# Sums of squares of three SSD groups formed inside the head loop, and rows of reciprocal roots taken through DRAM

## The reference

```
attn_out = rmsnorm(o.reshape(b, L, 2048), attn_norm_g) * silu(z_attn)      # o: 16 heads x 128
y = (y_f + y_b + d_skip * xs) * silu(z_ssm)                                # SSD, 32 heads x 64
y = rmsnorm(y.reshape(b, L, 4, 512), norm_g.reshape(4, -1))                # a mean of squares per group of 512 columns
mix = concatenate([attn_out, y]) @ w_out
out = x + rmsnorm(mix, post_norm_g)
```

## Time and profile before

| | |
|---|---|
| time, median of 3 executions | 2438.62 us (2438.27 to 2438.85) |
| the profiled execution's own time | 2437.44 us |
| its span, first to last instruction | 2435.6 us |
| granted clock of PE, mean | 0.998 |
| PE busy | 2405.2 us |
| PEld busy | 2284.6 us |
| DVE busy | 1744.1 us |
| ACT busy | 979.5 us |

### The profile page before, as it was taken

How to read it: one execution, slowest core, us unless ns; L and a number is a source line. 1 busy time by engine, 2 the same in 40 slices (tenths; PEclk the granted TensorE clock), 3 DMA queues, 4 the chain that set the end, 5 groups by cost and what they waited for, 6 DMA issues and landing times.

```text
span 2435.6 us, 37103 instructions
## 1 busy us (share of the span) xinstructions
PE 2405.2 (99%) x13708; PEld 2284.6 (94%) x13708; DVE 1744.1 (72%) x2435; ACT 979.5 (40%) x1622; POOL 387.4 (16%) x580
## 2 busy tenths in 40 slices
PE   7999999999999999999999999999999999999998
PEld 6999999999999999999999999999999988888887
DVE  5686766666666655554787888788878768787767
ACT  6323433333333333333445444544454533234332
POOL 0000267666676600000000000000000000000000
PEclk9999999999999999999999999999999999999999
DMA  4235466566556533335464546554654435443544
GB/s 162 78 108 161 132 193 193 185 190 193 185 188 185 179 95 95 99 100 205 145 188 143 180 144 186 171 152 144 193 163 134 143 113 179 156 156 120 170 167 157
DMA packets 316776, 379.43 MB, mean 156 GB/s; under 512 B 20006, under 2 KB 237286, under 8 KB 313751
## 3 DMA queue, kind: packets, MB, share of 16 engines
q1 hardware_dynamic: 265063, 222.06, 29.5%
q10 hardware_dynamic: 33200, 106.02, 13.0%
q0 software_dynamic: 18432, 50.36, 6.4%
HBM read 299.16 MB, written 86.54 MB: 158 GB/s over the span
## 4 chain that ended last, share of the span: by engine, by line
PE 95%; DMA 1%; DVE 1%; ACT 1%; issue 0%; ACTq 0%; SPq 0%; DVEq 0%
PE ps L1029 36%; PE ps L827 21%; PE ps L1182 14%; PE ps L805 8%; PE ps L1102 4%; PE ps L988 2%; PE ps L955 2%; PE ps L922 2%; PE ps L938 1%; PE ps L998 1%; DMA w_raw<-in_w_in 1%; PE ps L760 0%; PE ps L962 0%; PE ps L841 0%; PE ps L929 0%; PE ps L971 0%
## 5 line engine op out<-in xcount | busy, mean ns | idle before, releaser
L1029 PE MATMUL ps<-h_hi,w_hi 128*128 128x384 f32 x960 | 322.2, 336 | 0.0
L1029 PE MATMUL ps<-h_lo,w_hi 128*128 128x384 f32 x960 | 322.0, 335 | 0.0
L1029 PE MATMUL ps<-h_hi,w_lo 128*128 128x384 f32 x960 | 321.7, 335 | 0.0
L2211 DVE TENSOR_TENSOR w_lo<-raw_qk,w_hi 128x512 fp32r<-128x512 f32 x240 | 185.0, 771 | 180.4 <-ACT w_hi L1555 179.3
L827 PE MATMUL ps<-h_hi,w_hi 128*128 128x384 f32 x1056 | 275.1, 341 | 0.0
L1262 ACT ACTIVATE w_hi<-w_raw 128x512 fp32r<-128x512 f32 x176 | 110.0, 628 | 400.7 <-PE ps L827 270.7
L827 PE MATMUL ps<-h_lo,w_hi 128*128 128x384 f32 x1056 | 268.9, 335 | 0.0
L827 PE MATMUL ps<-h_hi,w_lo 128*128 128x384 f32 x1056 | 268.8, 335 | 0.0
L1029 PE MATMUL ps<-t_hi,w_lo 128*128 128x384 f32 x720 | 243.5, 338 | 0.0
L1029 PE MATMUL ps<-t_hi,w_hi 128*128 128x384 f32 x720 | 243.2, 338 | 0.0
L1029 PE MATMUL ps<-t_lo,w_hi 128*128 128x384 f32 x720 | 242.6, 337 | 0.0
(11 more groups left out here) (335 smaller groups left out, 5190.0 us busy)
## 6 DMA issues: line engine op xcount, KB each, us to landing
raw_qk<-in_w_in SPq DMA_DIRECT2D x90, 512.0 KB, 4.3
w_raw<-in_w_in SPq DMA_DIRECT2D x176, 256.0 KB, 3.6
stage<-loc_scr ACTq DMA_DIRECT2D x16, 1536.0 KB, 7.3
stage<-t_scr SPq DMA_DIRECT2D x48, 512.0 KB, 3.6
stage<-in_w_out SPq DMA_DIRECT2D x36, 512.0 KB, 3.5
stage<-zx_scr ACTq DMA_DIRECT2D x46, 384.0 KB, 9.0
stage<-in_w_in SPq DMA_DIRECT2D x30, 512.0 KB, 4.1
u_scr<-stage ACTq DMA_DIRECT2D x32, 384.0 KB, 2.6
```

What stands on the lines that cost most here:

```text
L1029: ins = nc.tensor.matmul(ps[:, bank, 0:HALF_T], w, h(k), start=(start and kk == 0 and q == 0), stop=(last and kk == KC - 1 and q == 2), sk ...
L2211: nc.vector.tensor_tensor(w_lo[:, n_slot(n, pp), :], src, w_hi[:, n_slot(n, pp), :].bitcast(f32), ALU.subtract).then_inc(w_lo_done, 1)
```

## The change

- **Squares in the loop.** For heads 0 to 11 (SSD groups 4, 5, 6), ACT squares y in step 1 of the next head, behind the exponentials of the sample (`square_of_y`): the first head of a group directly into the sum (two instructions), the others into `x_tok` (one instruction). DVE adds the others into the sum in step 2, between `pT_lo` and the decay exponents (`add_square_of_y`, two instructions). Before ACT copies the next x into `x_tok` in step 4 it waits for that addition. The sum lies in the triangles' place of `sq_c` and in `loc_ssum`.
- **Their sums over the partitions.** PE has them in slot 5 of the head behind the group's last (`group_sums`, three times), DVE forms the mean in step 6 (`group_mean`), PE waits for it before the next scores. One square root (ACT) and one reciprocal (DVE) after the last head serve all three.
- **PE's loop.** The iterations before it are 0 to 3, and the body holds four iterations and runs 3 times.
- **Rows.** Each of the four rows is stored to `r_scr` in DRAM (768 numbers from 128 partitions x 6) and loaded to all partitions (`store_root`, `load_root`, both on ACT's queue). `diagonals` and `roots_to_rows` are gone, so is ACT's copy.
- **Squares of group 7** stay where they were, but DVE adds one per unit, units 2 to 5, in place of two in unit 2 and two in unit 3.

```diff
-            def square_first(k):
...
+            def square_of_y(a):
+                if a % 4 == 0:
+                    if a == 0:
+                        for i in range(2):
+                            act.wait_ge(sum_a_out[i], 16 * SUM_TURNS)
+                        act.wait_ge(sum_d_out, 32 * SUM_TURNS)
+                    else:
+                        act.wait_ge(stat_ready, a // 4)
+                    nc.scalar.activation(ysum, y[:, 0:SEQ], ACT.Square)
+                    nc.scalar.activation(ysum_s, y[:, SEQ:T], ACT.Square).then_inc(y_squared, 1)
+                else:
+                    nc.scalar.activation(x_tok, y, ACT.Square).then_inc(y_squared, 1)
...
                 if a is not None and s == 1:
...
+                    if 1 <= a <= 4 * GROUP_STATS:
+                        square_of_y(a - 1)
...
+            def add_square_of_y(a):
+                dve.wait_ge(y_squared, X_DONE + a + 1)
+                did(nc.vector.tensor_tensor(ysum, ysum, x_tok[:, 0:SEQ], ALU.add))
+                nc.vector.tensor_tensor(ysum_s, ysum_s, x_tok[:, SEQ:T], ALU.add).then_inc(ysum_added, 1)
...
+                    if 1 <= a <= 4 * GROUP_STATS and (a - 1) % 4:
+                        add_square_of_y(a - 1)
                     decay_exponents(a)
...
+            def group_sums(g):
+                pe.wait_ge(ysum_added, X_DONE + 3 * g)
+                for t in range(TT):
+                    src = ysum[:, t * P:(t + 1) * P] if t < PCH else ysum_s[:, (t - PCH) * P:(t - PCH + 1) * P]
+                    last = nc.tensor.matmul(ps[:, 4, HALF_T + t:HALF_T + t + 1], src, ones[:, 0:1],
+                                            start=True, stop=True)
+                last.then_inc(stat_ready, 1)
...
-            iteration(1, 1, 0)
-            with pe.Fori(1, HEADS // 2) as g:
-                iteration(2 * g, 0, 2 * g - 1)
-                iteration(2 * g + 1, 1, 2 * g)
+            for i in range(1, 4):
+                iteration(i, i % 2, i - 1)
+            with pe.Fori(1, GROUP_STATS + 1) as g:
+                for q in range(4):
+                    iteration(4 * g + q, q % 2, 4 * g + (q - 1), (q, g))
...
-            def roots_to_rows(n, halves):
...
-            def diagonals(j, n, halves):
...
+            def store_root(j, n, stored):
+                act.wait_ge(r_ready, 1 if j < GROUP_STATS else j - GROUP_STATS + 2)
+                act.dma_start(r_scr[n].rearrange("(t p) -> p t", p=P), r_of(j), allow_slow_non_contiguous=True
+                              ).then_inc(stored, 16)
+            def load_root(n, row, came):
+                act.dma_start(row, r_scr[n:n + 1, :].rearrange("a t -> (a t)").partition_broadcast(P)).then_inc(came, 16)
...
+            store_root(STAT_SECOND, 0, r_stored)
+            store_root(STAT_THIRD, 1, r_stored)
             root(STAT_ATT)
+            store_root(STAT_ATT, 2, r_late_stored)
             w2_split(2)
             w2_split(3)
+            act.wait_ge(r_stored, 32)
+            act.wait_ge(w2_lo_done, 1)
+            load_root(0, r_rows[0], r_row_in)
+            load_root(1, r_rows[1], r_row_in)
+            act.wait_ge(r_late_stored, LATE_STORED + 16)
+            load_root(2, r_att_row, r_late_in)
...
+                    if step == 1 and p == 3 and i >= 2:
+                        add_square(1, 2, i - 2)
-                            if step == 1 and p == 3:
-                                add_square(1, 3, 2, k)
```

More of the change, by code:

```diff
@@ L909, in _, with slot @@
             QK_PASSES = ((q_hi, k_hi), (q_hi, k_lo), (q_lo, k_hi))
-            def slot(s, a, i):
+            def group_sums(g):
[5 more added lines that the diff above has]
+                last.then_inc(stat_ready, 1)
+            def slot(s, a, i, stat=None):
                 if a is not None and s == 0:
+                    if stat is not None and stat[0] == 2:
+                        pe.wait_ge(stat_read, stat[1])
                     pe.wait_ge(tile_out, tile_of(a, K) + 1)
@@ L973, in slot @@
                         last.then_inc(xt_ready, 1)
+                if s == 5 and stat is not None and stat[0] == 1:
+                    pe.wait_ge(xt_out, 2 * a + 2)
+                    group_sums(stat[1])
                 if a is not None and s == 6:
@@ L1108, in sums_of_squares @@
             def sums_of_squares(j):
-                if j == STAT_FIRST:
-                    pe.wait_ge(ssum_ready, 1)
-                elif j == STAT_ATT:
+                if j == STAT_ATT:
                     pe.wait_ge(att_gated, HEADS)
                 else:
[L1114 to L1119, removed]
+                    pe.wait_ge(ssum_ready, 1)
+                    pe.wait_ge(stat_read, STAT_LAST)
                 src = osq_sum if j == STAT_ATT else ssum
-                bank, at = (6, 0) if j == STAT_FIRST else (7, HALF_T)
                 for t in range(TT):
-                    last = nc.tensor.matmul(ps[:, bank, at + t:at + t + 1], src[:, t * P:(t + 1) * P], ones[:, 0:1],
+                    last = nc.tensor.matmul(ps[:, 7, HALF_T + t:HALF_T + t + 1], src[:, t * P:(t + 1) * P], ones[:, 0:1],
                                             start=True, stop=True)
                 last.then_inc(stat_ready, 1)
-            def roots_to_rows(n, halves):
[L1129 to L1132, removed]
             def first_step():
@@ L1688, in _ @@
             w2_split(1)
+            act.wait_ge(stat_read, GROUP_STATS)
+            nc.scalar.activation(r_cur[:, 0:GROUP_STATS, :], r_cur[:, 0:GROUP_STATS, :], ACT.Sqrt).then_inc(r_root, 1)
             store_y(HEADS - 1)
@@ L1693, in root, with squares_of @@
                 nc.scalar.activation(r_of(j), r_of(j), ACT.Sqrt).then_inc(r_root, 1)
-            def diagonals(j, n, halves):
[L1696 to L1707, removed]
+            def store_root(j, n, stored):
[4 more added lines that the diff above has]
+                act.dma_start(row, r_scr[n:n + 1, :].rearrange("a t -> (a t)").partition_broadcast(P)).then_inc(came, 16)
+            def squares_of(n, times):
                 act.wait_ge(u_buf_in[n], X_IN + 16 * times)
+                act.wait_ge(um_done, GRP)
                 for k in range(1, GRP):
-                    act.wait_ge(usq_added, (GRP - 1) * turn + k)
+                    act.wait_ge(usq_added, k)
                     nc.scalar.activation(usq, u_buf[n][:, k * T:(k + 1) * T], ACT.Square).then_inc(usq_done, 1)
@@ L1766, in _ @@
                         a_round(f + 1, h)
+                    if step == 1 and p == 5:
+                        act.wait_ge(r_late_stored, LATE_STORED + 32)
+                        act.wait_ge(um_done, 2 * GRP)
+                        load_root(3, r_rows[2], r_late_in)
                     if step == 1 and p == 3:
-                        squares_of(1, 3, 2)
+                        squares_of(1, 2)
                     for h in range(2, PHASE_B):
@@ L2173, in step @@
                     settle()
+                if s == 6 and a % 4 == 0 and 0 < a <= 4 * GROUP_STATS:
+                    group_mean(a // 4 - 1)
                 if s == 7:
@@ L2501, in _ @@
             mean_and_root(STAT_ATT)
-            for k in range(GRP):
-                add_square(0, 1, 1, k)
             w2_split(2)
@@ L2506, in _ @@
                 first_part(1, t)
-            mean_and_root(STAT_SECOND)
-            for k in range(GRP):
-                add_square(1, 2, 1, k)
             w2_split(3)
@@ L2523, in _ @@
                     for k in range(GRP):
-                        normalise(1, gb, k, row=2)
+                        normalise(1, gb, k, row=1)
                 if t >= 4:
@@ L2556, in _ @@
                             if step == 1 and p == 6:
-                                normalise(1, BLOCK_GROUPS[2][1], k, row=3)
+                                normalise(1, BLOCK_GROUPS[2][1], k, row=2, times=2)
                     if step == 1 and p == 4 and i == 2:
```

127 lines of the change are left out of this document (42 added, 85 removed).

## The result

The changed kernel takes 2449.91 us (median of 6 runs, 2448.84 to 2453.6) against 2438.44 for the kernel before in the same session: a ratio of 1.0054, 95% interval 1.0043 to 1.0064. It is slower by 11.5 us. The forecast was 2441.3, the range 2432 to 2447, with 0.21 on slower.

A forecast was written before the change was run, and what follows sets the result against it. PE, busy 99% of the span, was taken to bound the kernel. Terms of -7.25 (end part), +8.6 (head loop) and +1.3 (branches) gave +2.65 us on 2438.62, so 2441.3 us; range 2432 to 2447.

The forecast's parts named there:

- What PE no longer does: End part: four rows of roots leave PE, 6.35 us less; three sums of squares only move into the head loop, 0 net.
- the stall in the second pair: Second pair at the end: PE's wait for a unit that DVE adds late goes, 0.90 us less.
- The squares and the additions: Head loop: ACT's squares cost PE 5.9 us in 12 heads, DVE's additions 2.7 in nine; 8.6 us more.
- PE's longer loop: Two backward branches of the head loop: PE may fetch the doubled body again; 1.3 us taken between bounds 0 and 4.4.
- The prediction's own sign of being wrong: Head loop: the forecast is wrong if L955 shows no wait, or if either backward branch shows more than 2 us.
- backward branches: Rival, head loop: the body of four does not stay, two branches cost 2.2 us each; 2444.4 us, chance 0.16.
- What is hidden: End part: storing and loading the rows through DRAM costs PE nothing, with about 20 us of room for the first two.
- the rows come late: Rival, end part: storing 768 single numbers takes so long that group 5 is multiplied late; some 2446 us, chance 0.05.

The follow-up runs named there:

- experiment 9: Changed kernel with the edits of experiment 5, experiment 6, experiment 7 and experiment 8 together: 2430.27 us against 2438.03 for the kernel before, ratio 0.997.
- experiment 6: Changed kernel with only DVE's additions of squares moved behind the low part of the sample's probabilities: 2445.86 us against 2438.03 for the kernel before.
- experiment 7: Changed kernel with ACT's squares moved to step 2 and DVE's additions behind the low part of the sample's probabilities: 2439.3 us against 2438.03 before the change.
- experiment 1: Kernel before the change with only PE's loop over heads lengthened to four iterations, three passes: 2444.57 us against 2437.07, ratio 1.0031.
- experiment 2: Kernel before the change with only PE's loop lengthened to three iterations, 1947 PE instructions, four passes: 2449.66 us, ratio 1.0048.
- experiment 8: Changed kernel with the roots of groups 1 and 2 turned on PE and stored as 12 rows of 512 bytes: 2445.26 us against 2437.07 before the change.
- experiment 5: Changed kernel with PE's loop over heads written out in full, no backward branch between heads: 2440.13 us against 2437.07 for the kernel before, ratio 1.0014.

## Why the prediction was wrong

Two steps failed: the branch term was sized too low, and the rows through DRAM were taken as hidden. The method, to read each term from a row, held wherever there was a row of the thing itself. Step by step:

- *What PE no longer does* and *the stall in the second pair*: right. 7.25 us were forecast; experiment 9 has 7.5 for these terms and 7.28 in all. In the changed kernel itself the saving for group 6's row was lost to the wait below.
- *The squares and the additions*: right, 8.11 against 8.6 in sum, and experiments 6 and 7 take them away one by one. Head 0 was a good measure of what lateness costs there.
- *PE's longer loop*: the mechanism was named and the size was wrong. I took 1.3 us for two branches, between bounds of 0 and 4.4; they cost 7.1. Two faults are in that. The upper bound came from the transfer of 80 KB in the earlier trace rows (2.2 us), as if a stop were one such transfer. In experiments 1 and 2 PE stands 2.5 to 3.0 us each time; what that time is made of no run shows. And the value between the bounds leaned on the earlier trace rows, a loop that stays, which says nothing on a loop that doesn't. The lower clock at some of the stops, 1.6 us for a stretch of 3.4 us, I had not thought of at all. The prediction's own sign of being wrong, over 2 us at either branch, came true at both. The rival "backward branches" had the right cause, at 0.16 and with too low a price: with 7.1 in place of 4.4 it gives 2438.6 - 7.25 + 8.6 + 7.1 = 2447.1.
- *What is hidden*: wrong. The stores of 768 single numbers were priced by the row of another transfer. The second took 24.3 us, the load behind it 15.1, together twice the 20 us of room. PE paid 2.5 (the row's 1.29 not saved, 1.24 more) and 0.8 in the first pair, 3.3 in sum. The rival "the rows come late" had 0.05.

The two errors, 5.8 and 3.3 us, make 9.1; between the forecast's +2.65 and the measured +11.4 lie 8.8, as the other terms together came out 0.3 lower.

The Trainium skill (Runtime: NRT & Kernel Launch, Instruction fetch mechanics) says that a taken branch whose target isn't in the current window of two pages forces a fetch of that page before execution goes on. The stops at the branches agree, with 2.4 to 3.8 us each. The window doesn't: by the same section a page is 256 instructions, and the body of 1299 stays. The section's size of 2048 instructions for PE is not the length of a loop that stays either: bodies of 1587, 1779 and 1947 had to be fetched again in every pass. It is not disproved as a size: for 1587 instructions, 6.2 blocks of 256, the queue brings nine packets a pass, so more than the body is fetched. Whether this is why the body's start is no longer there no run shows.

What stays open: why the lower clock follows some stops and not others (1 of 2 in the changed kernel and in experiments 1, 6, 7 and 8, 3 of 3 in experiment 2, 6 of 6 with 1587 instructions, 1 of 6 with 1779); why the stops are 3.4 to 3.8 us with 1587 instructions and 2.4 to 3.0 elsewhere; where between 1299 and 1587 the limit lies; and whether one store of single numbers alone would have come in time.

## What to carry to other kernels

Keep a hardware loop of the bounding engine as short as one that is seen to stay, or write it out in full. Whether it stays is told by the instruction queue in the loop's second pass; if it does not, each backward branch cost a stop of 2.4 to 3.8 us here. Don't price a store of many single numbers by a transfer of another shape: here, beside other such stores and loads of weights, it took 15 to 32 us and held up the loads, and turning two columns to rows first cost PE 0.11 us. Work put on an engine just ahead of a hand-over without room costs most of its length (0.39 to 0.55 us of PE's time for a push of some 0.73 us); the same work behind the hand-over cost nothing.

## What the runs showed of the hardware

- A PE loop of 1299 instructions stays with the engine; of 1587, 1779, 1947 and 2595 (experiment 1) it is fetched again in every pass, and PE stands for 2.4 to 3.8 us at each backward branch. The same iterations as straight code (experiments 5 and 9) have no such stop.
- At such a stop PE's granted clock fell to 0.50 for 3.4 us (6.8 us at four of the six stops with 1587 instructions), in some cases and not in others. The fall came between 1.4 us before and 1.2 us after PE started again.
- Three stores of 768 single numbers, 3 KB each, issued within 5 us beside loads of weights, took 14.9, 24.3 and up to 32.2 us, with the 16 DMA engines at a busy share of 1.00 while these moved 174 GB/s; loads of 512 KB beside them took 16.0 us, and 8.1 with only the third of these stores left, which then took under 7 us.
